# A two-block transformer kernel: latent keys made in pairs, and another order of projections, attention units and output rows

## What is computed

```python
z = rms_norm_2(x, mix_norm[l]) @ w_mix_in[l]
z_mla, z_swa, z_na = jnp.split(z, [MLA_IN, MLA_IN + SWA_IN], axis=-1)
# mla_mixer: 8 heads, 64 own + 32 rotary channels
cq, ckv, k_rope = jnp.split(z_mla, [256, 384], axis=-1)
q = (rms_norm_2(cq, q_norm_g) @ w_uq).reshape(B, S, 8, 96)
kv = (rms_norm_2(ckv, kv_norm_g) @ w_ukv).reshape(B, S, 8, 64 + 64)
k_nope, v = jnp.split(kv, [64], axis=-1)
k = jnp.concatenate([k_nope, broadcast(k_rope)], axis=-1)
q, k = rms_norm_2(q, q_gain), rms_norm_2(k, k_gain)   # then rope on the last 32
o_mla = softmax(q k^T * 96 ** -0.5) v
```

## Time and profile before

| | us |
|---|---|
| runs, not profiled | 2973.7 median of 3 (2972.79 to 2974.1) |
| the profiled execution | 2973.22 |
| its span, first to last instruction | 2971.4 |
| PE busy | 2889.4 (97%), x13458 records |
| DVE, ACT, POOL busy | 1452.0, 1087.5, 223.9 |
| granted clock, mean | 0.988 |

### The profile page before, as it was taken

How to read it: one execution, slowest core, us unless ns; L and a number is a source line. 1 busy time by engine, 2 the same in 40 slices (tenths; PEclk the granted TensorE clock), 3 DMA queues, 4 the chain that set the end, 5 groups by cost and what they waited for, 6 DMA issues and landing times.

```text
span 2971.4 us, 36175 instructions
## 1 busy us (share of the span) xinstructions
PE 2889.4 (97%) x13458; PEld 2315.0 (78%) x13458; DVE 1452.0 (49%) x2090; ACT 1087.5 (37%) x1777; POOL 223.9 (8%) x166
## 2 busy tenths in 40 slices
PE   8999999999999999998999999999999999999998
PEld 5698777788788886677788888888886677788886
DVE  5673376543444434555454443544335655454432
ACT  4512343433332223655432222332224655433221
POOL 0000000000100021000120003000121001110011
PEclk9999999999999999999999999999999999999999
DMA  3201211134222322110222232223322111132232
GB/s 118 71 22 47 78 64 57 36 92 142 79 99 92 106 89 107 36 50 29 78 85 95 95 109 89 90 94 99 105 92 86 41 50 43 64 99 92 98 108 77
DMA packets 68364, 238.08 MB, mean 80 GB/s; under 512 B 10272, under 2 KB 12448, under 8 KB 67616
## 3 DMA queue, kind: packets, MB, share of 16 engines
q1 hardware_dynamic: 66240, 227.87, 23.3%
q10 hardware_dynamic: 2016, 8.77, 0.8%
HBM read 234.51 MB, written 2.10 MB: 80 GB/s over the span
## 4 chain that ended last, share of the span: by engine, by line
PE 68%; DVE 3%; ACT 2%; issue 1%; DVEq 0%; ACTq 0%
PE bank L381 19%; PE bank L383 19%; PE bank L382 19%; PE bank L860 3%; PE bank L886 2%; PE bank L665 2%; PE bank L872 2%; PE bank L638 1%; ACT L_probs L936 1%; DVE L_scores L984 1%; PE bank L1518 0%; PE bank L227 0%; ACT L_h_hi L1648 0%; PE bank L1461 0%; DVE L_area L1827 0%
## 5 line engine op out<-in xcount | busy, mean ns | idle before, releaser
L381 PE MATMUL bank<-L_h_hi,L_w_hi 128*128 128x512 f32 x1776 | 703.9, 396 | 6.1 <-DVE residual L1837 3.8
L382 PE MATMUL bank<-L_h_lo,L_w_hi 128*128 128x512 f32 x1776 | 692.2, 390 | 0.0
L383 PE MATMUL bank<-L_h_hi,L_weight_ring_low 128*128 128x512 f32 x1760 | 685.9, 390 | 0.0
L369 ACT CAST L_w_hi<-L_weight_ring 128x1024 fp32r<-128x1024 f32 (+2 forms) x290 | 324.1, 1118 | 909.5 <-PE bank L383 898.6
L375 DVE TENSOR_TENSOR L_weight_ring_low<-L_weight_ring,L_w_hi 128x1024 fp32r<-128x1024 f32 (+2 forms) x290 | 393.5, 1358 | 377.9 <-ACT L_w_hi L369 377.8
L381 PEld LDWEIGHTS bank<-L_h_hi,L_w_hi 128*128 128x128 f32 x1776 | 334.1, 188 | 82.2 <-issue 5.7
L382 PEld LDWEIGHTS bank<-L_h_lo,L_w_hi 128*128 128x128 f32 x1776 | 334.3, 188 | 74.2 <-issue 5.7
L383 PEld LDWEIGHTS bank<-L_h_hi,L_weight_ring_low 128*128 128x128 f32 x1760 | 330.6, 188 | 69.8
L381 PE MATMUL bank<-L_act_hi,L_w_hi 128*128 128x512 f32 x704 | 273.9, 389 | 0.0
L382 PE MATMUL bank<-L_act_lo,L_w_hi 128*128 128x512 f32 x704 | 273.9, 389 | 0.0
L383 PE MATMUL bank<-L_act_hi,L_weight_ring_low 128*128 128x512 f32 x704 | 273.9, 389 | 0.0
(11 more groups left out here) (338 smaller groups left out, 3874.4 us busy)
## 6 DMA issues: line engine op xcount, KB each, us to landing
L_weight_ring<-ffn_in SPq DMA_DIRECT2D x174, 512.0 KB, 3.3
L_weight_ring<-ffn_out SPq DMA_DIRECT2D x64, 704.0 KB, 4.1
B_weight_ring<-w_sqk SPq DMA_DIRECT2D x24, 512.0 KB, 3.3
B_weight_ring<-w_dn SPq DMA_DIRECT2D x16, 512.0 KB, 3.3
B_weight_ring<-w_gate SPq DMA_DIRECT2D x16, 512.0 KB, 3.3
L_weight_ring<-w_sna_qk SPq DMA_DIRECT2D x16, 512.0 KB, 3.3
L_weight_ring<-w_mix_out SPq DMA_DIRECT2D x16, 512.0 KB, 3.3
B_weight_ring<-w_sv SPq DMA_DIRECT2D x12, 512.0 KB, 3.3
```

The source lines that it names most:

```text
L369: e.copy(hv.high(at)[:, 0:width], hv.raw(sh, at)[:, 0:width]).then_inc(hv.w_hi_done, 1)
L381: e.matmul(out, a_hi, b_hi, start=start, stop=False)
L382: e.matmul(out, a_hi, b_lo, start=False, stop=False)
L383: return e.matmul(out, a_lo, b_hi, start=False, stop=stop)
```

## The change

Latent keys are projected for two heads at once: w_mla_k comes in four strips of 128 output rows, so that a layer has 12 latent jobs instead of 16: q0 k01 q1 q2 k23 q3 q4 k45 q5 q6 k67 q7. The sum of squares of a pair is taken with `ones64` (two blocks of 64 rows). The rotary key is summed once: ACT squares it into two row ranges of a tile of sh.sq, POOL zeroes the rows between, and for each pair POOL adds this tile to rows 0 to 95 of the job's squares before PE's sum, which waits for it (`sum_needs`). DVE writes the roped key to rows 32 to 95 of the other sh.sq tile, and finishes a pair with four products (64 own rows and 32 rotary rows for each head). PE's first job waits for three of the four latent results. The turns, written out:

The diff, with the renamed counts left out:

```diff
@@ -635,6 +635,8 @@
         e.wait_ge(jb.rstd, seen.free(jb.rstd) + fewer)
+        if "sum_needs" in job:
+            e.wait_ge(*job["sum_needs"])
         e.matmul(banks[sum_banks[b % len(sum_banks)]][:, 0:width], ones[0:kn, :], jb.sq[0:kn, b, 0:width], start=True,
@@ -764,6 +766,15 @@
                 e.wait_ge(jb.rstd, seen.ready(jb.rstd))
+                if "key_pair" in job:
+                    rope_key = job["rope_key"]
+                    for half, dest in enumerate(job["key_pair"]):
+                        own = slice(half * NOPE, (half + 1) * NOPE)
+                        rope = slice(32 + half * 32, 64 + half * 32)
+                        e.tensor_tensor(dest[0:NOPE, :], jb.g[own, b, :], jb.rs[own, b, :], ALU.mult)
+                        x = e.tensor_tensor(dest[NOPE:QK2, :], rope_key[rope, :], jb.rs[rope, b, :], ALU.mult)
+                    x.then_inc(jb.done, 1)
+                    continue
                 dests = [(job["dest"][0], slice(0, job["dest"][1]))] if "dest" in job else \
@@ -1159,6 +1170,8 @@
         kr_sq = sc.sem("rope_key_squared")
+        rope_added = sc.sem("rope_squares_added")
+        rope_zero = sc.sem("rope_squares_zero")
         oT_done = sc.sem("oT_done")
@@ -1194,7 +1207,9 @@
 
-        N_JOBS = 2 * MLA_HEADS + 8 + 4
+        N_MLA = MLA_HEADS + MLA_HEADS // 2
+        N_JOBS = N_MLA + 8 + 4
+        rope_key, rope_squares = sh.sq[:, 0, :], sh.sq[:, 1, :]
         H_PER, X_PER, O_PER = 4 * KT, 4 * KT, 10
@@ -1221,9 +1236,11 @@
                                      **({"needs": (v_done, layer * (2 * TT + 2) + TT + 1)} if h == 0 else {})))
-                mix_jobs.append(dict(parts=[[(0, ckv[:, 0, :])]],
-                                     rows=(0, NOPE), width=T, ones=(ones, QK2), scale=1.0 / QK2, gain=g("mlak"),
-                                     dest=(qk[:, tile + 1, :], QK2), split=False))
+                if h % 2 == 0:
+                    mix_jobs.append(dict(parts=[[(0, ckv[:, 0, :])]], rows=(0, P), width=T, ones=(ones64, P),
+                                         scale=1.0 / QK2, gain=g("mlak2"), split=False, rope_key=rope_key,
+                                         sum_needs=(rope_added, layer * (MLA_HEADS // 2) + h // 2 + 1),
+                                         key_pair=(qk[:, tile + 1, :], qk[:, tile + 3, :])))
 
@@ -1261,13 +1278,13 @@
                             v = lambda kt, h=h: v_mla[:, kt, h * MLA_V:(h + 1) * MLA_V]
-                            needs = [(jb.done, jobs_before + 2 * h + 2)] + (
+                            needs = [(jb.done, jobs_before + 3 * (h // 2) + 2 + h % 2)] + (
                                 [(v_done, layer * (2 * TT + 2) + 2 * TT)] if h == 0 else [])
...
                             k = qk[:, tile + 1, :]
-                            needs = [(jb.done, jobs_before + 2 * MLA_HEADS + tile + 2), (padded, layer * 8 + tile + 2)]
+                            needs = [(jb.done, jobs_before + N_MLA + tile + 2), (padded, layer * 8 + tile + 2)]
                         if kind in ("swa", "na"):
@@ -1296,26 +1313,27 @@
 
-        sums_first = range(6, 2 * MLA_HEADS + 8 + 1)
-        mix_turns = ["job"] * 5 + ["unit"]
-        for i in range(20):
-            mix_turns += ["unit"] + ["split"] * (i >= 10) + ["unit"] + {18: ["norm_used"]}.get(i, []) + ["job"]
-        mix_turns += ["unit", "unit", "row"] * 4
-        mix_turns += ["unit"] * 4 + ["norm", "unit"] * 3 + ["norm", "unit", "norm_used", "unit", "unit", "row"]
-        mix_turns += ["unit"] * 2 + ["row"] + ["unit"] * 4
+        sums_first = range(6, N_MLA + 8 + 1)
+        mix_turns = ["job"] * 4
+        job_after = (2, 4, 7, 9, 11, 15, 17, 19, 25, 27, 29, 32, 35, 39, 43, 46, 49)
+        split_after = (22, 24, 26, 28, 31, 34, 37, 41, 45, 48)
+        for u in range(1, 4 * TT * 4 + 2):
+            mix_turns += ["norm"] * (u in (54, 55, 56, 57)) + ["unit"] + ["split"] * (u in split_after)
+            mix_turns += ["norm"] * 4 * (u == 37) + ["norm_used"] * (u in (39, 57))
+            mix_turns += ["job"] * (u in job_after) + ["row"] * (u in (51, 53, 55, 57, 59, 61))
         act_turns, job = [], 0
...
                 if job in sums_first:
-                    act_turns += ["norm"] * (4 if job == 22 else 0) + ["job"]
+                    act_turns += ["job"]
                 job += 1
...
         v_at = 2 * FT + 2 * KT
-        sna_at = v_at + 4 + 5 + 2 * MLA_HEADS
+        sna_at = v_at + 4 + 5 + N_MLA
         mix_out_at = sna_at + 8
@@ -1379,11 +1397,10 @@
                     at = load_strip(e, seen, sh, at, A["w_mla_v"][layer])
-                    with seen.loop(e, MLA_HEADS // 4, free=[(sh.strip_done, 8)]) as it:
-                        for h in range(4):
-                            load_strip(e, seen, sh, at + 2 * h, A["w_mla_q"][layer, it * 4 + h])
-                            load_strip(e, seen, sh, at + 2 * h + 1, A["w_mla_k"][layer, it * 4 + h])
-                    at += 2 * MLA_HEADS
+                    for h in range(MLA_HEADS):
+                        at = load_strip(e, seen, sh, at, A["w_mla_q"][layer, h])
+                        if h % 2 == 0:
+                            at = load_strip(e, seen, sh, at, A["w_mla_k"][layer, h // 2])
                     assert at == at0 + sna_at
@@ -1462,7 +1479,7 @@
                     seen.ready(v_done, TT)
-                    e.wait_ge(lat_done, seen.ready(lat_done, 4))
+                    e.wait_ge(lat_done, seen.ready(lat_done, 4) - 1)
 
@@ -1611,8 +1628,9 @@
                     e.wait_ge(lat_scaled, 4 * layer + 4)
-                    e.activation(jb.sq[NOPE:QK2, 1, :], jb.g[NOPE:QK2, 0, :], ACT.Square).then_inc(kr_sq, 1)
                     latent_rstd(2, 1, cq_rstd)
+                    for rows in (slice(0, 32), slice(NOPE, QK2)):
+                        e.activation(rope_squares[rows, :], jb.g[NOPE:QK2, 0, :], ACT.Square).then_inc(kr_sq, 1)
                     e.wait_ge(sh.strip_done, seen.ready(sh.strip_done))
@@ -1771,7 +1789,7 @@
                     seen.ready(sh.strip_done)
-                    e.wait_ge(kr_sq, layer + 1)
+                    e.wait_ge(lat_scaled, 4 * layer + 4)
                     e.wait_ge(small, 64 * layer + 64)
@@ -1780,11 +1798,14 @@
                     e.wait_ge(lat_step, 3 * layer + 3)
-                    e.tensor_tensor(jb.g[lo, 1, :], jb.g[lo, 1, :], jb.tmp[lo, :], ALU.add).then_inc(lat_done, 1)
                     e.wait_ge(sh.rstd_done, seen.ready(sh.rstd_done))
...
                                                in1=cq_rstd, op0=ALU.mult, op1=ALU.mult).then_inc(lat_done, 1)
+                    e.wait_ge(kr_sq, 2 * layer + 2)
+                    e.tensor_tensor(rope_key[32:64, :], jb.g[lo, 1, :], jb.tmp[lo, :], ALU.add)
+                    e.tensor_tensor(rope_key[lo, :], jb.g[lo, 1, :], jb.tmp[lo, :], ALU.add).then_inc(lat_done, 1)
+                    e.wait_ge(lat_done, 4 * layer + 4)
 
@@ -1892,6 +1913,14 @@
                     norm_pool(e, seen, sh, xT)
+                    e.wait_ge(kr_sq, 2 * layer + 2)
+                    e.memset(rope_squares[32:64, :], 0.0).then_inc(rope_zero, 1)
+                    e.wait_ge(rope_zero, layer + 1)
+                    for p in range(MLA_HEADS // 2):
+                        j = 3 * p + 1
+                        e.wait_ge(jb.squared, layer * N_JOBS + j + 1)
+                        e.tensor_tensor(jb.sq[0:QK2, j % 2, :], jb.sq[0:QK2, j % 2, :], rope_squares[0:QK2, :],
+                                        ALU.add).then_inc(rope_added, 1)
                     e.wait_ge(small, 64 * layer + 64)
@@ -3087,7 +3116,7 @@
     ukv = a["mla_w_ukv_2"].reshape(L, P, MLA_HEADS, 128)
-    out["w_mla_k"] = np.moveaxis(ukv[..., :64], 2, 1)
+    out["w_mla_k"] = np.moveaxis(ukv[..., :64].reshape(L, P, MLA_HEADS // 2, P), 2, 1)
     out["w_mla_v"] = ukv[..., 64:].reshape(L, P, 512)
@@ -3102,7 +3131,7 @@
         two(a["swa_q_gain_2"]), two(a["swa_k_gain_2"]), two(a["na_q_gain_2"]), two(a["na_k_gain_2"]),
-        two(a["mem_q_gain_2"]), two(a["mem_k_gain_2"]),
+        two(a["mem_q_gain_2"]), two(a["mem_k_gain_2"]), two(a["mla_k_gain_2"][:, :64]),
         np.broadcast_to(a["swa_sink_2"][:, None, :], (L, P, 4))], -1)
```

10 lines of the change are left out of this document (5 added, 5 removed).

## The result

| | before | after |
|---|---|---|
| median of 5 runs each | 2973.46 (2972.47 to 2974.1) | 2997.83 (2986.97 to 3002.68) |
| the profiled execution, its span | 2973.22, 2971.4 | 3002.68, 3000.6 |
| granted clock, mean | 0.988 | 0.980 |
| PE busy, records | 2889.4, x13458 | 2901.4, x13426 |
| first job to output projection, layers 1 and 2 | 214.3 and 212.6 | 231.7 and 225.9 |

The ratio is 1.0079 (95% interval 1.0067 to 1.0091): 24 us slower, 12.8 above the upper end of the forecast's range. The time of a run goes with its clock: 2986.97 us is the run at 0.985, the four from 2997.2 to 3002.7 have 0.980 and 0.981. Outside the mixers nothing grew: the two stages are 17.4 and 13.2 us longer (30.7 together, unrounded), the profiled execution 29.5. That profiled execution is the slowest of the five, so its trace shows the loss at its largest.

What follows compares the result with a forecast made beforehand. PE, with no idle time from unit 4 to 41, bounds the kernel; -6.8 + 0.4 + 2.7 + 3.4 + 0.4 + 0.2 + 0.4 = +0.7 a layer, +1.4 in all, gives 2975 us, range 2963 to 2985.

Steps and rivals of the forecast that it cites:

- rival 2: Granted clock falls: four drops +5.4, GpSimd's upper end +3.2, 2984 us; excluded if unit 39's wait is under 1; chance 0.28.
- The saving of the pairs: Latent stretch on PE: two paired keys replace five key turns ahead of unit 4, 6.8 us a layer saved.
- The pair turn: PE time of one paired key with its sum in the latent stretch: 1.77 us.
- Unit 7: PE waits for an exponential because job 5 begins before finishing its predecessor, making rstd later: 1.7 us a layer.
- Unit 14: PE waits for an exponential behind job 8, delayed by the pair's four products: 0.5 us a layer.
- Unit 39: Group square sums on ACT delay the copy before PE's value matmuls: +3.4 us a layer (2.5 to 4).
- From unit 50 to the output projection: Last sixteen units with all six rows, to the output projection: near 31 us.
- The spread as such: Spread banded projections: split delay in units 40 to 43 +0.4 us, rows behind +0.2 (-3 to +3) a layer.
- rival 1: The cover holds: squares and pair products find gaps on ACT and DVE, 3.4 + 2.7 a layer vanish, 2963 us; chance 0.30.
- the head: First job to unit 4: later first maximum delays unit 4 by +0.4 us a layer (-0.5 to +2).
- GpSimd, "+0.4 (0 to 2)": Rope additions, then memory norm in mid-attention, delay DVE products: +0.4 us a layer (0 to 2).
- one of its signs: In the profile after, PE reaches the first banded projection about 4 us earlier in each layer.

Runs made afterwards that it cites:

- experiment 5: Kernel after, with GpSimd's memory norm before its rope additions, group squares in job 16's ACT turn, and job 4's sum ahead of job 5: 2967.23 us, ratio 0.9987.
- experiment 8: Paired keys, latent jobs spread after units 3 to 23, banded part as before, memory norm first, job 4's sum ahead of job 5: 2986.2 us, ratio 1.0054.
- experiment 11: experiment 5 with banded jobs, splits, norm steps and rows placed as in the kernel before: 2968.45 us, ratio 0.9987.
- experiment 4: Kernel before, single keys, with only the new order of the banded part (projections spread, squares and rows moved): 2983.72 us, ratio 1.0037.
- 7: Kernel after with GpSimd's memory norm first, plus four idle VectorE products ahead of unit 30's score mask: 2990.31 us, ratio 1.0067.
- experiment 13: Kernel after with memory norm first, seven idle VectorE products ahead of unit 20's maximum, job 11 moved from behind unit 19 to behind 22: 2997.95 us, ratio 1.0092.
- experiment 2: Kernel after with the four square sums of the first output group back on ACT inside job 16's turn: 2991.47 us, ratio 1.0064.
- experiment 6: Kernel after with GpSimd's memory norm first, plus two idle VectorE products ahead of unit 20's maximum: 3000.96 us, ratio 1.0096.
- experiment 3: Kernel after with paired keys only; banded jobs, splits, squares and rows placed as in the kernel before: 2989.0 us, ratio 1.0053.
- experiment 12: Kernel before with six idle VectorE products ahead of unit 20's maximum: 2974.72 us, ratio 1.0007.

## Why the prediction was wrong

It gave "slower" by a falling clock a chance of 0.28, but forecast no change; the time is outside its range, and past rival 2's own 2984 as well.

**Right, with the sizes of the terms.** The saving of the pairs: from unit 4 to unit 26 4.3 us a layer (77.0 before, 72.6 in experiment 5), and 2.0 of waits that came with it at units 7, 14 and 22, so some 6.3, predicted 6.8. The pair turn: 3.92 us from unit to unit with a pair's job and 2.14 without, 1.78, predicted 1.77. Unit 7: 3.79 instead of 2.14, 1.65, predicted 1.7. Unit 14: 2.73, 0.6, predicted 0.5. Unit 39: 4.9 us to the sum where version 5 has 1.7, 3.2, predicted 3.4. From unit 50 to the output projection 30.2 in both layers, predicted 31.1. The spread as such, without the squares: +0.4 us a layer by the trace of experiment 8 and +0.6 by that of experiment 11, predicted 0.4 + 0.2. Unit 8 to 20 and unit 26 to 39 hold no surprise. With the waits at these places taken away (experiment 5) the kernel is faster than before, as rival 1 had it, but by 5 us and not by 11 (2963 against 2973.7).

**The step that failed: rival 2's price of a fall of the clock.** The text said "9% of 20 us, 1.8 us for one drop", counted four of them, and made +5.4 of it; the forecast itself charged none. Three things were wrong in that step. First, the number of falls: unit 7 in both layers and unit 22 in both layers were not among the four places, though the waits there had been predicted, as 1.7 and 0.5 us. Second, the price is not one figure. The kernel before had one fall in its mixers, in the first layer's head, and I took its size for all. With version 5 as the reference (clock 1.00 from unit 4 on) and the waits taken off (1.4 at unit 22, 3.2 at unit 39), the clock alone cost 3.35 at unit 7, where job 6 follows, 1.4 at unit 39, where job 17 follows, and 9.4 (layer 1) and 3.0 (layer 2) at unit 22, where four units without a projection follow. At unit 39 it was 2.7 to 2.9 in three other cases (layer 1 of experiment 4, both layers of 7) and nothing in layer 1 of experiment 13. With a latent job behind the fall no loss was over 3.4 us (experiment 13, and all eleven falls at unit 7); without one it was over 9 in four cases of five. Third, the head: predicted +0.4, measured +1.6 and +3.8 (24.1 and 24.6 us to unit 4 against 22.5 and 20.8). The first scores came 11.1 us after the first job and the first transposes 16.2 us after it, near the steps' 11.0 and 15.9; but behind the 2.14 us wait and the one for the first exponential, what follows up to unit 4 took 8.0 us instead of 5.25, most of it at half clock. In layer 1 the kernel before has such a fall itself, so that only part is new. The sum: with 21.2 us as the prediction's own head, 2.9 + 3.35 + 9.4 + 1.4 less the 1.7 of before in layer 1, and 3.4 + 3.35 + 3.0 + 1.4 in layer 2, are 26.5 of the 30.7 us. The place that was to decide rival 2 was the wrong one too: "with that wait under 1 us it can't be", but in experiment 2 the wait at unit 39 is gone, and the median is still 18.9 us above the kernel before.

**The term that set it off: GpSimd, "+0.4 (0 to 2)".** It was charged as time on DVE, and by that it was inside its bounds: 1.4 us. Its place mattered, not its size. The memory norm fell on the products of the last pair, just ahead of the longest stretch without a job. The remaining 4.2 us of the 30.7 are about the forecast's 1.4 in all and this 1.4 in each layer. The Trainium skill (SBUF — State Buffer, "Who interferes with whom") has VectorE instructions with two SBUF inputs contend with GpSimd's reads, and calls the shared ports an exclusive lock; the prediction read that as whole instructions in turn. The trace agrees in kind and less in size: by whole instructions in turn a product would have taken 0.69 + 0.61, 1.30 us (an estimate); it took 1.00 to 1.12.

**Two smaller points.** The bounds of its terms add up to -7.4 and +9.6 us a layer, where it says -6 and +8; the measured 17.4 and 13.2 lie outside either. And one of its signs failed, that PE would reach the first banded projection about 4 us earlier: unit 26, right behind it, starts 111.7 and 105.8 us after the first job, against 99.5 and 97.8 before. It came true only without the waits, and by less: 97.0 us in both layers of experiment 5.

**What stays open.** Why the same wait lowers the clock one time and not another (1.82 us in experiment 2, 1.98 and 1.99 in the two layers of experiment 6), and why the low clock ended among mere units in layer 2 of the kernel after and not in layer 1. The last section has the counts over all traces, but they are too few for a chance; the spread of the runs (2986.5 to 3004.8 in experiment 6) shows that it falls differently from run to run. And the head: none of three orders removed its waits, so what the pairs would give with a head at full clock (an estimate: 3 us more a layer, by the difference of 24 and 21.2) was not shown.

## What to carry to other kernels

Where PE is full, price a new wait of 2 us or so not by its length but by what follows it: here 1.4 to 3.4 us where a projection came next, and up to 9.4, nearly the time of the whole stretch again, where only short matmuls followed. It may also cost nothing more, so take several executions. Look at the granted clock in the windows and at the start-to-start time of a repeated piece; the busy share says 100% either way. Before a change thins out such a stretch, put the waits of its head and the side work of GpSimd elsewhere: the same change went from +0.8% to -0.13% by three edits of order that removed no work.

## What was not expected of the hardware

- At the lower clock PE stays "busy", and can stay low: in layer 1 of the kernel after some 17 us of units 22 to 25 at 0.50, busy all the time, did not bring the clock back, and so in three other cases. In one case (layer 2) it was back after some 6 us of the same units. With one latent projection of four records and a sum behind the wait it was back each time, 3.4 us lost (experiment 13, both layers). The Trainium skill (TensorE: Matmul & The Clock Gate, "Why this matters for your kernels") names idle gaps between bursts as what lowers the clock, and continuous busy time as what brings TensorE to the full one; the fall behind a wait agrees, the 17 us of busy PE at 0.50 do not.
- A longer wait lowers the clock more often, but no length that was seen decides it. Counted over both layers of every trace, behind unit 4: 0.97 to 1.23 us at units 6, 7, 22 and 32, 0 of 8; 1.09 us at unit 43 with 0.42 more right behind it, 3 of 10 (experiment 3 in both layers, experiment 12 in layer 1); 1.48 us at unit 7, 11 of 15; 1.82 us at unit 22, 4 of 6; 1.98 us there (experiment 6), 1 of 2; 2.08 us at unit 16 (experiment 8), 1 of 2; 3.15 us at unit 39, 11 of 12; 3.11 and 3.18 us (experiments 13 and 8), 4 of 4.
- A product of DVE over 32 rows beside GpSimd took 1.00 us as one over 64 did (1.00 to 1.12), 0.68 and 0.69 alone; GpSimd's 256-column operations went from 0.61 and 0.73 to 1.06.
